# The last attention loop of a two-model kernel: transposes and weighing ahead of the scores on TensorE

## The reference

```python
# fox_attention, one block of 128 queries
logits = jnp.einsum('bhqd,bhkd->bhqk', qi, k).astype(jnp.float32) * scale
logits = logits + Fi[..., None] - F[:, :, None, :]
logits = jnp.where(causal, logits, -1e30)
p = jax.nn.softmax(logits, axis=-1)
return jnp.einsum('bhqk,bhkd->bhqd', p.astype(v.dtype), v)

# memory_attention
logits = jnp.einsum('bhqd,bhmd->bhqm', q, k).astype(jnp.float32) * scale
p = jax.nn.softmax(logits, axis=-1)
return jnp.einsum('bhqm,bhmd->bhqd', p.astype(v.dtype), v)
```

## Time and profile before

| | |
|---|---|
| median of 3 runs | 1484.4 us |
| span of the profiled execution | 1483.1 us (its first to its last instruction; the median of the runs is 1.3 us above it) |
| TensorE busy | 1452.5 us, 98% of the span |
| VectorE / ScalarE / GpSimd busy | 859.6 / 615.7 / 482.5 us |
| mean granted TensorE clock | 0.999 |
| the changed loop | from 1285.5 to about 1440 us of the span |

### The profile page before, as it was taken

The page is one execution under the profiler, slowest core; times in us unless marked ns, Lnnn a source line. Parts: engine busy times, 40 slices in busy tenths (PEclk is TensorE's granted clock), DMA queues, the critical chain, the costliest instruction groups (busy, mean ns, idle before and its releaser), DMA issues.

```text
span 1483.1 us, 23698 instructions
## 1 busy us (share of the span) xinstructions
PE 1452.5 (98%) x9390; PEld 1207.6 (81%) x9390; DVE 859.6 (58%) x1261; ACT 615.7 (42%) x780; POOL 482.5 (33%) x360
## 2 busy tenths in 40 slices
PE   8999999999999999999999999999999999999999
PEld 6787887898888888899777988888888897777677
DVE  7787686576665660165686666656630374565741
ACT  5565554353223221245574442232221355655541
POOL 0000000225544545432221145445454524422222
PEclk9999999999999999999999999999999999999999
DMA  7422122403222233323102122222323312322211
GB/s 222 136 74 87 58 86 102 156 29 114 85 92 106 87 112 113 112 87 106 66 30 86 57 86 85 95 103 88 110 85 112 129 58 86 130 74 71 72 56 59
DMA packets 23601, 137.25 MB, mean 93 GB/s; under 512 B 2600, under 2 KB 5208, under 8 KB 8672
## 3 DMA queue, kind: packets, MB, share of 16 engines
q1 hardware_dynamic: 18288, 124.79, 23.9%
q10 hardware_dynamic: 5232, 11.32, 2.8%
HBM read 131.89 MB, written 4.21 MB: 92 GB/s over the span
## 4 chain that ended last, share of the span: by engine, by line
issue 41%; PE 27%; POOL 24%; DVE 3%; DMA 2%; ACT 1%; DVEq 1%; POOLq 0%; ACTq 0%; SPq 0%
POOL WL L468 15%; POOL WL L477 9%; PE pair L503 7%; PE pair L505 6%; PE pair L504 6%; DMA RAW<-stream 1%; PE pair L1096 1%; PE pair L1083 1%; DVE WL L1672 1%; PE pair L688 1%; PE pair L1015 1%; PE pair L1073 1%; PE pair L717 1%; ACT WH L1202 1%; DMA PAR<-params 0%
## 5 line engine op out<-in xcount | busy, mean ns | idle before, releaser
L503 PE MATMUL pair<-AH,WH 128*128 128x512 f32 (+1 forms) x1240 | 473.4, 382 | 9.4 <-DVE AL L1661 6.6
L468 POOL TENSOR_TENSOR WL<-RAW,WH 128x512 fp32r<-128x512 f32 x228 | 310.5, 1394 | 475.6 <-ACT WH L1202 475.6
L505 PE MATMUL pair<-AH,WL 128*128 128x512 f32 (+1 forms) x1240 | 462.6, 373 | 0.0
L504 PE MATMUL pair<-AL,WH 128*128 128x512 f32 (+1 forms) x1240 | 462.4, 373 | 0.0
L1202 ACT ACTIVATE WH<-RAW 128x2048 fp32r<-128x2048 f32 x106 | 202.8, 1913 | 455.5 <-PE pair L505 446.4
L477 POOL TENSOR_TENSOR WL<-RAW,WH 128x512 fp32r<-128x512 f32 x128 | 171.8, 1374 | 506.8 <-ACT WH L1202 506.8
L503 PEld LDWEIGHTS pair<-AH,WH 128*128 128x128 f32 x1240 | 233.5, 188 | 58.5 <-issue 15.9
L505 PEld LDWEIGHTS pair<-AH,WL 128*128 128x128 f32 x1240 | 233.0, 188 | 41.8
L504 PEld LDWEIGHTS pair<-AL,WH 128*128 128x128 f32 x1240 | 233.5, 188 | 41.1 <-issue 1.9
L2042 DVE TENSOR_SCALAR CA<-pair,PAR 128x512 f32<-128x512 f32 x88 | 67.3, 806 | 147.4 <-PE pair L505 144.4
L503 PE MATMUL pair<-GH,WH 128*128 (+2 forms) x416 | 148.7, 357 | 0.1
(11 more groups left out here) (249 smaller groups left out, 1890.4 us busy)
## 6 DMA issues: line engine op xcount, KB each, us to landing
RAW<-stream SPq DMA_DIRECT2D x114, 1024.0 KB, 4.9
H<-x_t SPq DMA_DIRECT2D x5, 512.0 KB, 6.6
bias_rows<-ROWS ACTq DMA_DIRECT2D x1, 2048.0 KB, 24.5
BIAS<-bias_rows ACTq DMA_DIRECT2D x1, 2048.0 KB, 7.8
FBC<-forget_rows ACTq DMA_DIRECT2D x4, 512.0 KB, 4.0
out<-H ACTq DMA_DIRECT2D x8, 256.0 KB, 2.0
H<-x_t SPq DMA_DIRECT2D x1, 1024.0 KB, 10.4
RAW<-stream SPq DMA_DIRECT2D x3, 256.0 KB, 6.7
```

The source lines that it names most:

```text
L468: pool.tensor_tensor(WL[w][:, part], RAW[raw][:, part], WH[w][:, part].bitcast(F32), ALU.subtract).then_inc(w_lo, 1)
L503: pe.matmul(out_, wh, xh, start=start, stop=False, skip_group_check=shared)
L504: pe.matmul(out_, wh, xl, start=False, stop=False, skip_group_check=shared)
L505: return pe.matmul(out_, wl, xh, start=False, stop=stop, skip_group_check=shared)
```

## The change

In TensorE's loop over u, `score(u + 2)` moves from ahead of `turn(u)` to behind `weigh(u - 1)`. The filler stays where it is, behind all three. No instruction is added or taken away and no other engine's stream changes.

```diff
@@ -1142,11 +1142,11 @@
             query_key(0, 1)
             head_sum(3)
             for u in range(20):
-                if u + 2 < 20:
-                    score(u + 2)
                 turn(u)
                 if u:
                     weigh(u - 1)
+                if u + 2 < 20:
+                    score(u + 2)
                 if u == 0:
                     head_sum(4)
                     pe.wait_ge(n_made, 4)
```

## The result

| | before | changed |
|---|---|---|
| median | 1484.53 us (20 runs, 1483.49 to 1489.65) | 1488.78 us (20 runs, 1486.02 to 1491.51) |
| ratio, 95% interval | | 1.0024 (1.0018 to 1.003) |
| span of the profiled execution | 1483.1 us | 1486.2 us |

The ratio makes 3.6 us, 2.7 to 4.5. The prediction had 1486.4, range 1484.0 to 1489.2; the time lies in the range, above its likeliest value, and its middle on the slower side of the 0.2% bound (the interval, 0.18 to 0.30%, includes it). To slower I had given 0.39, to within the bound 0.57.

A forecast was written before the change was run, and what follows sets the result against it. The prediction took TensorE, working 98% of the span, as the bound. Its terms, 0.96 + 1.26 + 1.59 - 0.5 - 1.26 = +2.05 us, took the median from 1484.4 to 1486.4 us, range 1484.0 to 1489.2.

The forecast's parts named there:

- (a): At u = 1, 7 and 11 scores no longer fill the wait for late weights: +0.96, then +0.63 twice, 1.26.
- (b): Everything that starts from a score starts later: at u = 15 +1.59 us, at u = 17 and 18 -0.5.
- the gate: At u = 17 and 18 the fourth gate is ready earlier, final product at 1430.7 instead of 1431.20: -0.5 us.
- (c): Other switches between kinds of matmul save 0.14 us at each of nine units: -1.26, kept from 0 to -2.5.
- The collision rival: At u = 5, 9 and 13 VectorE's mask meets GpSimd, slack becomes waits, switches save nothing: about +4.2, 1488.6 us; chance 0.24.
- The clock rival: Idle stretch at u = 15 drops the clock to 1.2 GHz, slowing the following filler: +7.5 us, 1491.9; chance 0.03.
- four signs of being wrong: Transposes wait at u = 5, 9 or 13; weighing-to-scores over 0.1 us dearer; clock falls behind u = 15; 1, 7, 11 lose nothing.

## Why the prediction was right, and where it fell short

**(a) Late transposes, +0.96 and +1.26.** Right. The filler of u = 1 starts 13.60 us behind the head sum (1299.38 - 1285.78) and started 12.67 behind it, +0.93. u = 7 and 11 lose their scores' length: the loop of the kernel with the new order up to 11 is within 0.03 us of the sum. The prediction's list of the new waits (1.0, 1.3, 1.3, 2.9 and 1) fits the five that came; its total of 5.5 us is a slip, for they add up to 7.5, and 7.5 was measured.

**(b) u = 15, +1.59, and the gate, -0.5.** Right. To the filler of u = 15 the sum of terms was 0.96 + 1.26 + 1.59 less eight savings of 0.14, 2.69; the trace has 2.62 (1415.33 - 1285.78 against 126.93). At the start of the final product it is 1.97, 0.65 less, where I had 0.5 and one more saving.

**(c) Switches, 0.14 a unit.** Right: filler to transposes is 0.23, and the switch from weighing to scores, which no row had shown, costs as much as the others:

```profile
1407.52 0.39 PE L505 MATMUL pair<-AH,WL 128*128 128x512 f32 x1
1407.75 0.82 PE L1083 MATMUL pair<-CON,PL 128*128 128x128 f32 x6
1408.49 0.67 PE L1096 MATMUL pair<-PT,VF 128*64 128x128 f32 x8
```

with the scores at 1409.09, 0.60 behind the start of that weighing. Filler stood 0.59 behind a weighing of that size in the kernel before. The Trainium skill (TensorEngine Tiling (Array Packing), Key Properties) says that a change of tiling mode drains TensorE. The trace agrees in sign: one change fewer, 0.14 us less.

**The collision rival** did not come. At u = 9 the logits of unit 10 start later by what I had said, and inside GpSimd's low part, yet VectorE's mask (L2232) is not stretched, and the head norm ends at 1366.46, 1 us before the filler asks for it:

```profile
1359.08 5.28 POOL L468 TENSOR_TENSOR WL<-RAW,WH 128x512 fp32r<-128x512 f32 x4 [10.78 <-ACT WH L1202]
1359.20 0.96 DVE L2229 SCALAR_TENSOR_TENSOR PL<-pair,FBC 128x768 f32<-128x768 f32 x1 [5.87 <-PE pair L1073]
1360.23 0.42 DVE L2232 TENSOR_TENSOR PL<-PL,CON 128x256 f32<-128x256 f32 x1
...
1365.72 0.74 DVE L2160 SCALAR_TENSOR_TENSOR QKN<-pair,PAR,RH 128x512 f32<-128x512 f32 x1
```

At u = 5 the mask does take 0.86 us, 0.43 more than in the kernel before. What neither I nor the rival had counted is that an operation behind it, the cast L2257, takes 0.43 us now where it took 1.33 before, so VectorE loses nothing in sum (changed, then before):

```profile
1325.52 0.86 DVE L2232 TENSOR_TENSOR PL<-PL,CON 128x256 f32<-128x256 f32 x1
1330.34 0.43 DVE L2257 CAST OH<-CON 128x512 fp32r<-128x512 f32 x1
...
1327.03 1.33 DVE L2257 CAST OH<-CON 128x512 fp32r<-128x512 f32 x1
```

**The clock rival** is the step that was mis-sized, in chance and in price. I gave it 0.03 and took two things as evidence against it. One was that the first 5 us show a clock of 1.00 with TensorE idle; that row says nothing of an idle stretch between busy ones. The other was that the trace shows no fall at all, and that is a misreading: the kernel before had one at 245 us, behind a wait of 2.31 us, in the very trace, and its mean clock of 0.999 instead of 1.000 was the sign of it. That place also bounds the price, since the clock is back within 5 us there. At u = 15 it is 1.5 us and not 5.45: I had slowed a whole filler, and the execution that shows it was at the lower level only from about 1411.6 to 1415.0.

The Trainium skill (TensorE: Matmul & The Clock Gate, part 1) has the clock halve after an idle stretch. The traces agree on the halving, at waits of 1.95 to 4.53 us at u = 15, but it does not come in every execution. The forecast's sum plus a price of 1.5 us would have been 1487.9, where the ratio puts the time at 1488.1.

**How much of the hit was luck.** The mechanism of the order was right, to 0.1 us of the loop. That the time fell into the range was in part luck: the range reached up to 1489.2 to hold the collision, which did not come, and left out the clock, which did and lies a good 1.5 us above the likeliest value. Of the prediction's own four signs of being wrong one came true, the clock behind u = 15.

That the +3.6 us are these two and nothing else rests on the loop of 1.96, measured, the one execution of the changed kernel with 1.52, and the mean clocks. How often the clock falls at u = 15 was not seen run by run, since only the profiled executions have a trace: four of the five with a wait of 1.95 us or more there show it, and the means cannot be read place by place.

## What to carry to other kernels

When work is moved off the place in front of a wait, ask what covers that wait then: here scores of 0.6 to 1.1 us were the cover, and moving them turned 3.7 us of idle time into 7.5. Put in front of a wait what depends on it least and is needed last: with the weighing of the unit before in that place, the waits of the kernel before fell from 3.7 us to 2.7, and to 1.2 with two units ordered apart. The larger part of those two gains (3.1 of 4.1 us, 3.4 of 5.9) came from another source, transposes that stand right before filler, so count waits and switches apart before you credit one. And when small waits merge into one of 2 to 3 us on a TensorE that is otherwise busy, add the price of a clock that falls, in part of the runs; look for such a wait elsewhere in the trace of before, with the granted clock behind it.

## What was not expected of the hardware

A wait of 3.0 us of TensorE cost 1.5 us more than itself in one profiled execution and 2.6 in another (the new order from u = 12), through a granted clock of 0.50, and one of 1.95 us cost 1.6; the runs' clocks and times say that this is common. One profiled execution need not show it: the first of the changed kernel has the same wait and the clock at 1.00 (windows view),

```profile
1410.00:1415.00 5.00, 2.40 (x22) 2.07 (x24) 2.22 (x6) 4.90 (x10) 0.00 (x0) 1.00 0.00 0
```

and only the runs' times and mean clocks pointed there. And transposes were cheapest right next to the big matmuls: eight of them take 0.85 us ahead of filler and 1.02 between scores and weighing.
